# Second block's head: norm squares summed on VectorE, index weights and forget logits taken into neighbouring products, key heads computed once, rotary rows turned by DMA

## The reference, cut to what matters

```python
h = _rmsnorm(x, g_mix)
proj = h @ w_in                       # 7244 columns
qa, ka, va, qb, kb, vb, fl, qc, kc, vc, qi, ki, wi, gl = split(proj)
br_a = stick_breaking(qa, ka, va)     # 8 heads of 64
br_b = forgetting(qb, kb, vb, log_sigmoid(fl + b_forget))     # fl: 8 columns
qc, kc, qi, ki = rope of each         # 8, 2, 4, 1 heads: the first 16 of 64 channels are rotated
br_c = indexed_sparse(qc, kc, vc, qi, ki, wi, top_k=64)       # wi: 4 columns
y = sigmoid(gl)[0] * (br_a @ w_b[0]) + ...                    # three branches
x = x + y @ w_out
x = x + square(relu(_rmsnorm(x, g_mlp) @ w_up)) @ w_down
```

## Time and profile before

| | us |
|---|---|
| time, median of 3 runs (lowest, highest) | 1583.32 (1579.73, 1584.66) |
| the profiled execution: span from first to last instruction | 1580.8 |
| the profiled execution's own time | not listed apart; the 1580.8 stand for it |
| PE busy | 1510.2 (96%) |
| DVE busy | 798.2 (50%) |
| ACT busy | 337.2 (21%) |
| POOL busy | 276.5 (17%) |
| first layer's head, first raw product to first product of qa | 544.84 to 600.42 |
| second layer's head, the same | 1062.15 to 1112.93 |
| DMA, mean busy share in 600 to 760 | 0.40 |

### The profile page before, as it was taken

One profiled execution on the slowest core, in us unless ns is written; L12 is line 12 of the kernel. 1 busy time (PEld: TensorE's weight loads), 2 busy tenths in 40 slices (PEclk: granted clock), 3 DMA queues, 4 the chain that ended last, 5 costly groups with the idle time before them and its releaser, 6 DMA issues.

```text
span 1580.8 us, 31295 instructions
## 1 busy us (share of the span) xinstructions
PE 1510.2 (96%) x13635; PEld 1310.4 (83%) x13635; DVE 798.2 (50%) x1491; ACT 337.2 (21%) x719; POOL 276.5 (17%) x145
## 2 busy tenths in 40 slices
PE   7999999798789899999999999999999999999998
PEld 2667758686678688998988999998899888899987
DVE  2342344655652426667531866522666753186653
ACT  1102133534432401033400121000103340012100
POOL 3404001000000035663200000003576220000000
PEclk9999999899899999999999999999999999999999
DMA  9312240000011534433434444463443333444451
GB/s 349 118 60 100 91 150 4 2 3 20 2 56 55 135 107 158 162 108 110 152 116 157 160 160 160 168 176 112 160 161 107 121 147 117 150 160 161 160 184 69
DMA packets 110904, 191.63 MB, mean 121 GB/s; under 512 B 20888, under 2 KB 27296, under 8 KB 110640
## 3 DMA queue, kind: packets, MB, share of 16 engines
q1 hardware_dynamic: 109776, 188.29, 34.7%
q0 software_dynamic: 960, 1.33, 0.3%
q10 hardware_dynamic: 32, 0.01, 0.0%
HBM read 188.57 MB, written 1.05 MB: 120 GB/s over the span
## 4 chain that ended last, share of the span: by engine, by line
PE 87%; DVE 3%; PEld 3%; issue 2%; ACT 2%; DMA 2%; DVEq 1%; ACTq 1%; SPq 0%; PEldq 0%
PE psum L1410 16%; PE psum L1260 15%; PE psum L1235 13%; PE psum L1407 6%; PE psum L867 4%; PE psum L1527 3%; PE psum L1256 3%; PEld psum L1546 2%; PE psum L1462 2%; PE psum L951 2%; PE psum L942 2%; PE psum L1118 2%; PE psum L1546 2%; PE psum L1566 1%; PE psum L1331 1%
## 5 line engine op out<-in xcount | busy, mean ns | idle before, releaser
L1260 PEld LDWEIGHTS psum<-arena 128*128 128x128 f32 x2240 | 254.3, 192 | 8.7 <-issue 8.0
L1260 PE MATMUL psum<-arena 128*128 128x128 f32 x2240 | 260.9, 276 | 0.0
L1999 ACT ACTIVATE arena<-psum 128x512 f32<-128x512 f32 (+6 forms) x242 | 116.4, 495 | 642.2 <-PE psum L1260 118.3
L1410 PEld LDWEIGHTS psum<-arena 128*128 128x128 f32 x2240 | 250.4, 192 | 0.1
L1410 PE MATMUL psum<-arena 128*128 128x128 f32 x2240 | 250.5, 274 | 0.0
L1235 PE MATMUL psum<-arena 128*128 128x256 f32 x928 | 202.9, 379 | 0.0
L1235 PEld LDWEIGHTS psum<-arena 128*128 128x128 f32 x928 | 175.2, 189 | 25.5 <-issue 0.3
L820 POOL TENSOR_TENSOR arena<-arena 128x1024 f32<-128x1024 f32 x12 | 28.3, 2355 | 565.3 <-DMA arena<-in_w_in 514.7
L1407 PE MATMUL psum<-arena 128*128 128x256 f32 x448 | 97.0, 379 | 0.0
L1407 PEld LDWEIGHTS psum<-arena 128*128 128x128 f32 x448 | 84.9, 190 | 11.9
L1546 PE MATMUL psum<-arena 128*128 128x256 f32 x336 | 73.4, 379 | 0.8 <-issue 0.8
(11 more groups left out here) (399 smaller groups left out, 2060.4 us busy)
## 6 DMA issues: line engine op xcount, KB each, us to landing
arena<-in_w_in SPq DMA_DIRECT2D x33, 2048.0 KB, 7.8
arena<-in_w_up SPq DMA_DIRECT2D x16, 2048.0 KB, 8.4
arena<-in_w_down SPq DMA_DIRECT2D x16, 2048.0 KB, 7.8
arena<-in_w_out SPq DMA_DIRECT2D x6, 2048.0 KB, 8.3
arena<-in_w_branch SPq DMA_DIRECT2D x6, 2048.0 KB, 7.5
arena<-in_mod_w SPq DMA_DIRECT2D x5, 2048.0 KB, 13.9
arena<-in_w_in SPq DMA_DIRECT2D x3, 1024.0 KB, 6.7
arena<-in_w_in SPq DMA_DIRECT2D x12, 256.0 KB, 4.7
```

The costliest lines, as they stand in the source:

```text
L1260: mm = pe.matmul(b[:, n * P:(n + 1) * P], left[:, k, n * P:(n + 1) * P], right[:, k, :], start=k == 0, stop=k == half - 1)
L1410: mm = pe.matmul(b[:, n * P:(n + 1) * P], left[:, k, n * P:(n + 1) * P], right[:, k, :], start=first and n == 0 and k == 0, stop=last and ...
L1999: return act.activation(dst, src, ACT.Copy, scale=scale)
```

## The change

It has five parts.

1. The squares of the norms: DVE adds the eight tiles of squares up in seven additions (`squares_summed`), in ss1 and in ss2, and PE multiplies the sum once. `raw_tiles` now goes tile k by tile k over all four output tiles; the one product of the norm stands behind the k below 5 in layer 0 and below 3 elsewhere.
2. fl (8 columns) and ki (64) stand in one tile of weights with ki, "kf": ki in partitions 0 to 63, the logits in 64 to 71, and the 56 columns behind are not used. wi's four columns stand behind vc's 128. Chunk 2 holds 132 columns now.
3. kc is one tile, each key head in one half. Two DMAs from SP make the swapped copy for the later score products.
4. The five products with `rot` go, and its table. The frequency table has a sign, so that sin has it. ACT issues four DMAs of 8 rows over qc, qi and kc, which lie side by side (7 x 256 columns), into `turned_rows`; one that doubles ki; and four of ki's rows. DVE multiplies and adds over 128 x 1792 at once.
5. The forget logs are made in 8 rows, and one DMA from SP doubles them. ACT copies vc and wi out behind the forget logs.

SP's new waits stand ahead of chunk 7 (for `roped`) and ahead of chunk 8 (for `forget_ready`). Lines that only move memory are left out of the diff.

```diff
-            [(0, 3592, 64), (64, 3592, 64), (128, 3656, 64), (192, 3656, 64), (256, 3848, 256)],
-            [(0, 3720, 128), (128, 4104, 64), (192, 4104, 64), (256, 4168, 4), (260, 3072, 8), (324, 3072, 8)],
+            [(0, 3592, 128), (128, 3848, 256), (384, 4104, 64), (448, 3072, 64)],
+            [(0, 3720, 128), (128, 4168, 4)],
...
-CHUNK_ENDS = (["qc1", "qi", "fl"] + [f"{x}_4" for x in HEAD_PARTS] + [f"gl{n}_4" for n in range(GATES)]
+CHUNK_ENDS = (["qc1", "kf", "vc"] + [f"{x}_4" for x in HEAD_PARTS] + [f"gl{n}_4" for n in range(GATES)]
...
+                        if i == 7:
+                            sp.wait_ge(sem("roped"), l + 1)
+                            sp.dma_start(kc[0:HALF, 1, :], kc[HALF:P, 0, :]).then_inc(sem("keys_swapped"), 16)
+                            sp.dma_start(kc[HALF:P, 1, :], kc[0:HALF, 0, :]).then_inc(sem("keys_swapped"), 16)
+                        if i == 8:
+                            sp.wait_ge(sem("forget_ready"), l + 1)
+                            sp.dma_start(fn[0:8, :], fn[FOX, :]).then_inc(sem("forget_doubled"), 16)
...
-            for k in range(KT):
+            pe.wait_ge(sem(ready), l + 1)
+            pe.matmul(v[:, 0:T], cst("ones"), sq[:, 0, :], start=True, stop=True).then_inc(b.filled, 1)
+
+        def raw_tiles(pe, pieces, ks, ready, l):
+
+            for k in ks:
                 pe.wait_ge(sem(ready), l * KT + k + 1)
-                mm = pe.matmul(v[:, 0:T], cst("ones"), sq[:, k, :], start=k == 0, stop=k == KT - 1)
-            mm.then_inc(b.filled, 1)
-
-        def raw_tiles(pe, pieces, ks, ready, l):
-
-            for b, w, c0 in pieces:
-                for i in range(2):
-                    for k in ks:
-                        pe.wait_ge(sem(ready), l * KT + k + 1)
+                for b, w, c0 in pieces:
+                    for i in range(2):
                         mm = pe.matmul(b[:, i * T:(i + 1) * T], w[:, k, c0 + i * P:c0 + (i + 1) * P], raw[:, k, :],
                                        start=k == 0 and i == 0, stop=k == KT - 1, skip_group_check=True)
-                if k == KT - 1:
-                    mm.then_inc(ly.filled, 1)
+                    if k == KT - 1:
+                        mm.then_inc(ly.filled, 1)
...
-            raw_tiles(pe, pieces, range(0, KT - 2), "raw1_ready", l)
-            norm_sum(pe, take_bank, ly, "ss1", "squares1", l)
-            raw_tiles(pe, pieces, range(KT - 2, KT), "raw1_ready", l)
+            summed_by = 3 if l else 5
+            raw_tiles(pe, pieces, range(0, summed_by), "raw1_ready", l)
+            norm_sum(pe, take_bank, ly, "ss1", "squares1_summed", l)
+            raw_tiles(pe, pieces, range(summed_by, KT), "raw1_ready", l)
             w = use_chunk(pe, n0 + 1, l)
-            tiles("kc", w, (0, P), src=raw)
-            tiles("qi", w, (2 * P, 3 * P), src=raw)
+            tiles("kc", w, (0,), src=raw)
+            tiles("qi", w, (P, 2 * P), src=raw)
+            tiles("kf", w, (3 * P,), ready=lambda k: pe.wait_ge(sem("h1_ready"), l * KT + k + 1))
             w = use_chunk(pe, n0 + 2, l)
-            pe.wait_ge(sem("h1_ready"), l * KT + KT)
-            tokens("vc", w, 0, P)
-            tiles("ki", w, (P,))
-            tokens("wi", w, 2 * P, 4)
-            b = take_bank(ly, "fl", l)
-            for k in range(KT):
-                mm = pe.matmul(b[0:FOX_ROWS, 0:T], w[:, k, 260:260 + FOX_ROWS], ht[:, k, :], start=k == 0, stop=k == KT - 1)
-            mm.then_inc(ly.filled, 1)
-
-            pe.wait_ge(sem("const2_landed"), 16)
-            for g, of, src in (("rqc0", "qc0", qc[:, 0:2]), ("rqc1", "qc1", qc[:, 2:4]), ("rkc", "kc", kc), ("rqi", "qi", qi)):
-                ly.wait_emptied(pe, of, l)
-                b = take_bank(ly, g, l)
-                pe.matmul(b, cst("rot"), src.rearrange("p a t -> p (a t)"), start=True, stop=True).then_inc(ly.filled, 1)
-            ly.wait_emptied(pe, "ki", l)
-            b = take_bank(ly, "rki", l)
-            pe.matmul(b[:, 0:T], cst("rot"), ki, start=True, stop=True).then_inc(ly.filled, 1)
+            tokens("vc", w, 0, VC)
...
+                    pe.wait_ge(sem("const2_landed"), 16)
...
-                        pe.wait_ge(sem("forget_ready"), l + 1)
+                        pe.wait_ge(sem("forget_doubled"), 16 * (l + 1))
                     q = {"A": qa, "B": qb, "C": qc}[kind][:, p]
-                    kk = kc[:, p // 2] if kind == "C" else {"A": ka, "B": kb}[kind][:, p]
+                    kk = [kc[:, p // 2 ^ x] if kind == "C" else {"A": ka, "B": kb}[kind][:, p] for x in range(2)]
+                    if i == "BAC".index("C") * HEADS // 2:
+                        pe.wait_ge(sem("keys_swapped"), 32 * (l + 1))
...
-            raw_tiles(pe, pieces, range(0, KT - 2), "raw2_ready", l)
-            norm_sum(pe, take_bank, ly, "ss2", "squares2", l)
-            raw_tiles(pe, pieces, range(KT - 2, KT), "raw2_ready", l)
+            raw_tiles(pe, pieces, range(0, 3), "raw2_ready", l)
+            norm_sum(pe, take_bank, ly, "ss2", "squares2_summed", l)
+            raw_tiles(pe, pieces, range(3, KT), "raw2_ready", l)
...
-            out_of("kc", kc)
+            out_of("kc", kc[:, 0], n=1)
             out_of("qi", qi)
-            ly.wait_filled(act, "vc", l)
-            emptied(ly, copy(vc, bank(ly, "vc", l)[:, 0:T].rearrange("p (m n) -> p m n", m=2)))
-            out_of("ki", ki, n=1)
-
-            ly.wait_filled(act, "fl", l)
-            f8 = slice(0, FOX_ROWS)
-            emptied(ly, act.activation(fs[f8], bank(ly, "fl", l)[f8, 0:T], ACT.Identity, bias=bf[f8, l:l + 1]))
             act.drain()
+            for r in (0, HALF):
+                for s in (0, 8):
+                    act.dma_start(turned_rows[r + s:r + s + 8], roped_rows[r + 8 - s:r + 16 - s]).then_inc(sem("queries_turned"), 16)
+            ly.wait_filled(act, "kf", l)
+            copy(ki[0:HALF], bank(ly, "kf", l)[0:HALF, 0:T])
+            emptied(ly, act.activation(fs[FOX], bank(ly, "kf", l)[FOX, 0:T], ACT.Identity, bias=bf[FOX, l:l + 1]))
+            act.drain()
+            act.dma_start(ki[HALF:P], ki[0:HALF]).then_inc(sem("index_keys_turned"), 16)
+            for r in (0, HALF):
+                for s in (0, 8):
+                    act.dma_start(turned_ki[r + s:r + s + 8], ki[8 - s:16 - s]).then_inc(sem("index_keys_turned"), 16)
+            f8 = FOX
             act.activation(fe[f8], fs[f8], ACT.Abs)
             act.drain()
             act.activation(fe[f8], fe[f8], ACT.Exp, scale=-1.0)
             act.drain()
             act.activation(fe[f8], fe[f8], ACT.Ln, bias=one_[f8])
             done("forget_logs")
+            ly.wait_filled(act, "vc", l)
+            b = bank(ly, "vc", l)[:, 0:2 * VC].rearrange("p (m n) -> p m n", m=2)
+            copy(wi, b[:, :, P:VC], 0.5)
+            emptied(ly, copy(vc, b[:, :, 0:P]))
...
+        def squares_summed(dve, done, fence, name, l, pairs):
+
+            for n in pairs:
+                dve.wait_ge(sem(name), l * KT + 2 * n + 2)
+                dve.tensor_tensor(sq[:, 2 * n, :], sq[:, 2 * n, :], sq[:, 2 * n + 1, :], ALU.add)
+                fence()
+                if n:
+                    dve.tensor_tensor(sq[:, 0, :], sq[:, 0, :], sq[:, 2 * n, :], ALU.add)
+                if n == 3:
+                    done(name + "_summed")
...
+            squares_summed(dve, done, fence, "squares1", 0, range(4))
             for k in range(KT):
-                dve.wait_ge(sem("squares1"), k + 1)
...
+            if l:
+                squares_summed(dve, done, fence, "squares1", l, range(4))
...
-            ly.wait_filled(dve, "wi", l)
-            emptied(ly, dve.tensor_scalar(wi, bank(ly, "wi", l)[:, 0:8].rearrange("p (m h) -> p m h", h=4), 0.5, None, ALU.mult))
-
-            dve.wait_ge(sem("const2_landed"), 16)
-            parts = (("rqc0", qc[:, 0:2], 2, 0), ("rqc1", qc[:, 2:4], 2, 512), ("rkc", kc, 2, 1024), ("rqi", qi, 2, 1536), ("rki", ki.unsqueeze(1), 1, 2048))
-            for g, x, n, o in parts:
-                ly.wait_filled(dve, g, l)
-                emptied(ly, dve.tensor_tensor(blocks_of(rotated[:, o:o + n * T], T), blocks_of(bank(ly, g, l)[:, 0:n * T], T),
-                                              bc(sin if g == "rki" else sinr, n), ALU.mult))
-            for g, x, n, o in parts:
-                dve.tensor_tensor(x, x, bc(cos if g == "rki" else cosr, n), ALU.mult)
-            fence()
-            for g, x, n, o in parts:
-                dve.tensor_tensor(x, x, blocks_of(rotated[:, o:o + n * T], T), ALU.add)
+            rows7, turned7 = blocks_of(roped_rows, T), blocks_of(turned_rows, T)
+            dve.wait_ge(sem("queries_turned"), 64 * (l + 1))
+            dve.tensor_tensor(turned7, turned7, bc(sinr, 7), ALU.mult)
+            dve.tensor_tensor(rows7, rows7, bc(cosr, 7), ALU.mult)
+            dve.wait_ge(sem("index_keys_turned"), 80 * (l + 1))
+            dve.tensor_tensor(turned_ki, turned_ki, sin, ALU.mult)
+            dve.tensor_tensor(ki, ki, cos, ALU.mult)
```

(15 more changed lines are left out.)

34 lines of the change are left out of this document (17 added, 17 removed).

## The result

The changed kernel takes 1541.0 us (median of 4 runs, 1536.42 to 1543.86), the kernel before 1581.53 in the runs beside it: a ratio of 0.9748, 95% interval 0.9726 to 0.9769. It is faster; forecast were 1537.7 and a range of 1531 to 1549. The profiled execution took 1543.86, 1542.1 of it in the span, against 1580.8: 38.7 less where the working gave 45.6. So the sign and the place were right, and 7 us of the sum did not arrive. The median lies in its range; the profiled span lies just outside the 1532 to 1542 that were given for it.

The account below looks back on a forecast made before the run. PE was taken to bound the kernel; 12.1 + 6.9 + 8.1 - 0.2 + 18.7 = 45.6 us leave it, so 1580.8 - 45.6 = 1535.2 profiled, plus 2.5 for a median of 1537.7, range 1531 to 1549.

Parts of the forecast that it names:

- What bounds the kernel: Whole kernel: PE, busy 96% of the span; work leaving PE's program leaves the time unless a wait replaces it.
- rival 3: Parts after the head bound by DVE or POOL keep half of parts 2 to 4, 16.7 us: 1554.4; 4 in 100.
- signs of being wrong: Prediction wrong if PE waits in qa or ka, the clock falls in a new place, or the gates' stretch grows.
- Norms (12.1): Four norms: eight PE products become one, 3.03 us saved each, 12.1 in all; DVE's additions covered by 0.5 to 2.
- kc (6.9): Heads of both layers: 8 of kc's 16 products go, 3.47 us a layer, 6.9 saved.
- wi (8.1), vc (-0.2): Both heads: wi's own products go, 3.49 and 4.57 us, 8.1 saved; its columns on vc cost 0.11 a layer.
- fl and the rotation (18.7): Both heads: these products leave PE, 18.7 us saved; fl dear because wi's 4-column products lower PE's clock.
- First products of layer 0 (nothing): Layer 0's first raw products: no gain taken, PE's clock being halved; bounds 3.2 us gained, 1.7 lost.
- The rotation's `roped` at +7, price nothing: From qa's start: `roped` at +7 (5.7 to 11.2), PE needs the bank at +16.1; cover 9 us, late 4.5.
- rival 1: Head gets a new wait: POOL's additions hold DVE's rotary operations, PE stalls 4.4 to 6.4 a layer, 1546.5 to 1550; 13 in 100.
- POOL's sums for ka: ka's second product: POOL's first two sums at +11.1 from qa's start, needed at +14.3; cover 3.2 us.
- SP's waits: Ahead of chunks 7 and 8: SP's waits for `roped` and `forget_ready` cost nothing.

Follow-up runs that it names:

- experiment 1: Kernel before with part 1 alone (squares added on DVE, one norm product, raw products tile by tile): 1566.08 us, ratio 0.9905; second measurement 1567.17 us.
- experiment 6: Changed kernel with the rotation's products back on PE, no row DMAs, ki in 64 partitions: 1543.28 us, ratio 0.9761 against the kernel before.
- experiment 3: Changed kernel without POOL's additions for ka's chunk, so ka is not computed: 1537.83 us, ratio 0.9725 against the kernel before.
- experiment 4: Changed kernel with the 1792-column addition ahead of the wait for ki's rows: 1533.69 us, ratio 0.97; again 1534.5 us, ratio 0.9727.
- experiment 5: Changed kernel with ki rotated in 64 partitions only, 1536.7 us; the same with the wide addition ahead of the wait for ki's rows, 1536.2 us.
- half ki: Changed kernel with ki rotated in 64 partitions only, three ACT issues fewer, SP doubling ki later: 1536.7 us, ratio 0.9716 against the kernel before.
- both remedies: Changed kernel with ki rotated in 64 partitions only and the wide addition ahead of the wait for ki's rows: 1536.2 us, ratio 0.9713.

## Why the prediction was right, and where it was off

- **What bounds the kernel.** Right: PE's removed work left the time nearly one for one, and rival 3 did not come: from va on, the rest is as long as it was less the norms, but for 2.5 us (below). Two of the prediction's own signs of being wrong did come, though: PE waits in ka, and the clock falls in a new place. The stretch with the gates did not grow, but it lost 0.55 where 3.03 were due. PE's busy time went down by 43.9, forecast 45.
- **Norms (12.1).** Right: experiment 1 has them, and in the changed kernel the second norms with their raw products take 14.27 and 14.26 us where they took 17.32 and 17.33, 3.05 and 3.07 less; forecast were 3.03 each. DVE's sum was covered but in one place, where PE waits 0.26 (at 556.96); the cover there was put at 0.5 or more.
- **kc (6.9).** Right within the heads: 64 instructions of L1239 hold kc, qi and kf in 13.87 us, 32 products at 0.433.
- **wi (8.1), vc (-0.2).** The first was read from a row of layer 0 that a fall of the clock had lengthened (4.57); at full clock wi is 3.49, 7.0 in two layers. vc pays 0.02 a layer, not 0.11.
- **fl and the rotation (18.7).** The rows of the one profile were right for that profile, the reason was too strong: with wi ahead fl was dear in five of ten passes, not each time. At full clock fl and the rotation are 3.51 + 3.87 = 7.38 a layer, and over the three profiles of before the clock adds 5.0, 3.3 and 3.3, counting wi's part. With wi the three come to 21.7 at full clock and 25.0 to 26.7 as they ran, against 26.8 forecast.
- **First products of layer 0 (nothing).** Mis-sized. From first raw product to kc it is 14.88 us where it was 20.0 to 20.5, of which one norm explains 3.03: 2.1 to 2.6 gained, near the bound of 3.2. I took the clock's fall there as given; in the changed kernel's profile the granted clock is 1.00 from the first product on, and in the new order it fell in experiments 1 (once in two) and 6 only. What decides it was not found.
- **The rotation's `roped` at +7, price nothing.** This is the step that failed. It came at +16.6 and +14.8. Issues were right (0.68 us each, the 0.58 of the earlier trace rows and a gap). The landing of ki's rows was +5.9, inside the bounds of +2.4 to +7.9 but not the +3.6 taken; and the 3.3 us behind it became 10.7 and 9.1, since all four operations in layer 0 and three in layer 1 were held by additions of POOL's. The 2.0 us of fixed time cited there from the Trainium skill (DMA: Bandwidth & Descriptors, Anatomy of one DMA) are given for DMAs that GpSimd issues; behind ACT's last issue the rows here took 2.7 us (the queries) and 5.2 (ki). That is rival 1's mechanism, to which I gave 13 in 100. Its place (ka's third product) was right in layer 0; in layer 1, where `roped` comes ahead of the +16.1, the loss is at ka's second product and the index scores. Its size was smaller than its own sum: 2.88 and 1.15 us instead of 4.4 to 6.4 a layer. Experiment 3 shows the cause in layer 0, experiments 4 and 5 two ways out. The clause "cover: 9 us" was reckoned on rates of DVE alone, though the earlier trace rows had an operation at five times its rate beside POOL.
- **POOL's sums for ka.** Forecast +11.1 against a need of +14.3. The chunk landed at +5.2 and +5.8 instead of +4.1, and in layer 1 an addition was itself lengthened by DVE's, to 4.13 us; PE waited 0.29 at 1090.69. The margin of 3.2 was just used up there; in layer 0 the sums came at +12.4.
- **SP's waits.** Nothing, as said. `roped` held SP until 596.82, but its next load was issued only at 606.66.
- **What is left open.** The stretch between va and layer 1's head is 434.6 us in both profiles of the changed kernel and in experiments 3 and 6, 432.0 in both profiles of experiment 4 and 432.3 with half ki (432.1 due). With both remedies it is 434.0. In the four long ones the clock drops once, somewhere between 721 and 737 us, right behind a wait of PE's of 1.4 to 1.8 us; the kernel before has such a wait (1.46) without the drop, and so has experiment 4. They also wait 0.6 us for ACT some 20 us later, and where the long wait is under 1.8 another 0.3 for DVE. In the changed kernel the extra waits are 0.9 us and the lower clock carries the rest of the 2.6, about 1.7. With both remedies the clock does not drop, and PE waits 1.96 for ACT instead. It does not hang on the waits at ka: experiment 3 has none and is long, and there layer 1 has a wait of 2.32 for ACT as well, as far behind va as the waits for ACT here, with a fall of the clock behind it: 3.8 us more than in the changed kernel. I did not find what decides it; it carries 2.5 us, also of what experiments 4 and 5 gain. The 2.97 us ahead of the first raw product are no cost of the change: in its second profile that point is at 543.91.

So 45.6 less 4.0 of waits at ka, 2.5 of that stretch, 3.0 of the first block and plus 2.6 of layer 0's head gives 38.7. The median fared better, 3.3 above the forecast: it was put 2.5 above the profiled span and lies 1.1 below it, since the profiled execution was the slowest of its four. That is luck. It is luck too that the misses of the sum partly cancel: the waits at ka, priced at nothing, cost 4.0, and the first products of layer 0, priced at nothing as well, gave 2.6.

## What to carry to other kernels

When work leaves the busiest engine for another one, cost its new chain as it will stand beside its neighbours, not alone: beside GpSimd's additions an operation with two inputs in SBUF that takes 0.4 us alone is to be counted at 2 to 2.6, one that takes 2 at about 4, and a chain of four such eats most of a cover of nine. Put whatever does not need the late operand ahead of the wait for it; here one moved line took away the same waits as leaving GpSimd's work out. A clock fall seen in one profile is a sample: take a second profile before pricing the work behind it.
